# Up projections of both MLPs with tokens as rows, and the squares turned by VectorE in 32x32 blocks

## The chip, the cores and the metric

The kernel runs on one core of a Trainium2 chip. The metric is the device time of one execution in microseconds (us). Engines are named TensorE (PE in profiles), VectorE (DVE), ScalarE (ACT), GpSimd (POOL) and SyncE (SP, which here issues the loads of weights).

## The reference

Two transformer-like layers run one after the other over 256 tokens (S) of width 2048 (D), all in float32. The first mixes a state-space block and an indexed attention, the second a compressed/selected/windowed attention and a gated delta rule. Each ends in an MLP of the same form, which is what the change is about:

```
# first layer                                     # second layer
u = rmsnorm(x, g_mlp) @ w_up                      h = rms_norm(x, ln2_w)
x + jnp.square(jax.nn.relu(u)) @ w_down           x + jnp.square(jax.nn.relu(h @ w_up)) @ w_down
```

w_up is 2048 x 8192, w_down is 8192 x 2048. The result of the second layer goes through one more RMS norm.

## The kernel before, in words

**Products in two parts.** Every float32 factor is split into hi (rounded to fp32r, which TensorE multiplies) and lo (what is left). A product is hi*hi + hi*lo + lo*hi. Activations are held as hi and lo side by side, as tiles of 128 features x 256 tokens (h or mix, [P, 2, 16 * 256]).

**Weights in units.** SyncE loads weights in pieces of 128 x 2048 into a ring of 4 (weight_ring). A piece is two units of 128 x 1024. For each unit ScalarE writes w_hi (a cast, L2115 in split_to) and VectorE then writes w_lo (a subtraction, L1262). There are 4 slots for units (UNITS = 4): ScalarE can cast unit n only when TensorE is done with unit n - 4 (semaphore unit_used), and TensorE takes unit n when VectorE has written its lo (unit_lo). On both engines split_to(unit + UNITS) stands at the head of each step of a stage, and the other work of the step behind it, so an instruction's place in this written order decides what it holds up.

**The MLP's stages.** Each MLP runs in four rounds f = 0 to 3. A round's up stage makes 2048 of the 8192 hidden features, its down stage multiplies them with 2048 rows of w_down and adds to the tokens' x. Each stage takes 32 units, 16 pieces.

- *Up stage before*: features as rows. project -> column -> products_of_two (L531 to L537) keeps 128 x 128 of the weights stationary and moves the activations: 512 columns (hi and lo of 256 tokens) under w_hi, 256 columns (hi) under w_lo. A tile of 128 features is done in two units, and lands in one of banks 0 to 2: hi*hi + lo*hi in the left half and hi*lo in the right. ScalarE lifts the right half (L2121), VectorE adds the left (L1282); for each pair of tiles VectorE does max(.,0) times the norm's 1/root (L1650), ScalarE squares (L2424) and casts the hi part (L2426), VectorE subtracts for the lo part (L1658).
- *Down stage*: tokens as rows. products_moving (L539 to L545) keeps a 128 x 128 piece of the activations stationary (hi, hi, lo) and moves 512 columns of the weights (hi, lo, hi). A block is 512 output features for all 256 tokens; it takes 8 units and two banks (128 tokens each), alternately 3 and 4 or 5 and 6. VectorE adds each bank to the tokens' x (L1726).

The gain of the norm is multiplied in ahead of the up stage (h = x * gain), the 1/root of the mean square behind it. The sum of squares comes from TensorE (folded_norm) as 256 columns, the same on all partitions. In the second MLP the first up stage also turns x into tokens as rows (turned_x: 8 times 4 transposes on TensorE, copied by ScalarE).

## Time and profile before

| | us |
|---|---|
| median of 3 runs | 2675.21 |
| lowest, highest | 2672.89, 2678.63 |
| the profiled execution, its own time | 2677.62 |
| its span | 2675.8 |

| engine | busy us | share of the span | instructions |
|---|---|---|---|
| PE (TensorE, products) | 2642.0 | 99% | 14484 |
| PEld (TensorE, loading what is stationary) | 2274.5 | 85% | 14484 |
| DVE | 1741.5 | 65% | 2361 |
| ACT | 1322.5 | 49% | 1903 |
| POOL | 208.0 | 8% | 182 |

The profile shows one execution. A matmul's recorded length reaches beyond the start of the next one, since they are pipelined, so TensorE's pace is read from the starts of instructions and not from their lengths. The same holds, to a smaller degree, for VectorE and ScalarE. The time of the profiled execution is 1.8 us above its span.

### The profile page before, as it was taken

The numbers are of one execution on the slowest core, as the hardware profiler recorded it, in microseconds if no ns is written. First come the engines' busy times: TensorE is split into PE (matmuls) and PEld (weight loads), VectorE is DVE, ScalarE is ACT, GpSimd is POOL, SyncE is SP. The second block draws the span as 40 slices with busy tenths as digits, with TensorE's granted clock in tenths as the row PEclk, the third lists the DMA queues.
The fourth block names the chain that finished last, engine by engine and source line by source line (L and its number), as shares of the span: only waits on it lengthen the run. The fifth ranks groups of instructions, "written<-read, shape, count | busy, mean of one in ns | idle before, by whom it ended". The sixth has DMA issues, their size and how long they took to land. (4 is left out here: it accounts for less than half of the span.)

```text
span 2675.8 us, 35946 instructions
## 1 busy us (share of the span) xinstructions
PE 2642.0 (99%) x14484; PEld 2274.5 (85%) x14484; DVE 1741.5 (65%) x2361; ACT 1322.5 (49%) x1903; POOL 208.0 (8%) x182
## 2 busy tenths in 40 slices
PE   9999999999999999999999999999999999999998
PEld 8778888888888888888889888988888888888887
DVE  7888796555556555785776767566665555565555
ACT  6545455535445344565554545455555354454454
POOL 3014001000000000140411300000000000000000
PEclk9999999999999999999999999999999999999999
DMA  7644445555555555566333333355555555555553
GB/s 269 165 166 158 164 167 189 189 191 186 198 181 189 203 186 194 186 251 241 142 133 137 125 127 113 131 198 189 189 197 186 198 188 191 189 189 193 185 200 130
DMA packets 68174, 481.91 MB, mean 180 GB/s; under 512 B 8008, under 2 KB 8136, under 8 KB 11177
## 3 DMA queue, kind: packets, MB, share of 16 engines
q1 hardware_dynamic: 65520, 467.43, 48.8%
q0 software_dynamic: 1968, 10.75, 1.5%
q8 instruction: 115, 1.88, 0.3%
q10 hardware_dynamic: 520, 1.43, 0.1%
q14 instruction: 51, 0.41, 0.0%
HBM read 473.29 MB, written 6.29 MB: 179 GB/s over the span
## 5 line engine op out<-in xcount | busy, mean ns | idle before, releaser
L1262 DVE TENSOR_TENSOR w_lo<-weight_ring,w_hi 128x1024 fp32r<-128x1024 f32 x882 | 1083.2, 1238 | 697.8 <-ACT w_hi L2115 696.7
L2115 ACT CAST w_hi<-weight_ring 128x1024 fp32r<-128x1024 f32 x884 | 916.4, 1048 | 646.0 <-PE bank L545 408.9
L533 PE MATMUL bank<-h,w_hi 128*128 128x512 f32 x2848 | 906.9, 400 | 0.0
L536 PEld LDWEIGHTS bank<-h,w_lo 128*128 128x128 f32 x2848 | 535.9, 188 | 126.6
L533 PE MATMUL bank<-mix,w_hi 128*128 128x512 f32 x1776 | 569.8, 402 | 4.1 <-DVE w_lo L1262 1.9
L536 PE MATMUL bank<-h,w_lo 128*128 128x256 f32 x2848 | 560.8, 278 | 0.0
L533 PEld LDWEIGHTS bank<-h,w_hi 128*128 128x128 f32 x2848 | 437.2, 189 | 7.7 <-issue 5.7
L543 PE MATMUL bank<-w_hi,mix 128*128 128x512 f32 x1056 | 411.2, 389 | 0.0
L544 PE MATMUL bank<-w_lo,mix 128*128 128x512 f32 x1056 | 410.9, 389 | 0.0
L545 PE MATMUL bank<-w_hi,mix 128*128 128x512 f32 x1056 | 410.8, 389 | 0.0
L536 PEld LDWEIGHTS bank<-mix,w_lo 128*128 128x128 f32 x1776 | 335.2, 189 | 79.3
L536 PE MATMUL bank<-mix,w_lo 128*128 128x256 f32 x1776 | 350.9, 279 | 0.0
L533 PEld LDWEIGHTS bank<-mix,w_hi 128*128 128x128 f32 x1776 | 272.9, 190 | 7.2 <-DVE w_lo L1262 2.1
L2121 ACT COPY arena<-bank 128x256 f32<-128x256 f32 x274 | 101.6, 372 | 357.3 <-PE bank L536 343.6
L543 PEld LDWEIGHTS bank<-w_hi,mix 128*128 128x128 f32 x1056 | 198.2, 188 | 41.0
L544 PEld LDWEIGHTS bank<-w_lo,mix 128*128 128x128 f32 x1056 | 198.2, 188 | 40.9
L545 PEld LDWEIGHTS bank<-w_hi,mix 128*128 128x128 f32 x1056 | 198.2, 188 | 40.7
L1282 DVE TENSOR_TENSOR arena<-arena,bank 128x256 f32<-128x256 f32 x272 | 113.4, 418 | 130.3 <-ACT arena L2121 130.1
L2797 POOL TENSOR_TENSOR arena<-arena 128x512 f32<-128x512 f32 x28 | 41.6, 1486 | 1067.3 <-ACT arena L2183 1066.5
L2424 ACT ACTIVATE arena<-arena 128x512 f32<-128x512 f32 x64 | 40.4, 632 | 87.9 <-DVE arena L1650 87.9
L1658 DVE TENSOR_TENSOR mix<-arena,mix 128x512 fp32r<-128x512 f32 x64 | 43.9, 685 | 10.8 <-ACT mix L2426 10.8
L1650 DVE SCALAR_TENSOR_TENSOR arena<-arena 128x512 f32<-128x512 f32 x64 | 44.3, 692 | 6.5
(369 smaller groups left out, 1758.9 us busy)
## 6 DMA issues: line engine op xcount, KB each, us to landing
weight_ring<-in_w_up SPq DMA_DIRECT2D x128, 1024.0 KB, 4.8
weight_ring<-in_w_down SPq DMA_DIRECT2D x128, 1024.0 KB, 4.8
weight_ring<-in_w_merge SPq DMA_DIRECT2D x32, 1024.0 KB, 4.8
weight_ring<-in_w_gdn SPq DMA_DIRECT2D x24, 1024.0 KB, 4.8
weight_ring<-in_w_papb SPq DMA_DIRECT2D x16, 1024.0 KB, 4.8
weight_ring<-in_w_o SPq DMA_DIRECT2D x16, 1024.0 KB, 4.8
weight_ring<-in_w_xbc SPq DMA_DIRECT2D x12, 1024.0 KB, 4.8
weight_ring<-in_w_q SPq DMA_DIRECT2D x8, 1024.0 KB, 4.8
```

Source lines behind the costliest of these rows:

```text
L533: e.matmul(bank[:, :], w_hi[:, unit_at % UNITS, o + j * P:o + (j + 1) * P], x[:, :, at + j * S:at + (j + 1) * S], start=first and j == 0, ...
L536: done = e.matmul(bank[:, 0:S], w_lo[:, unit_at % UNITS, o + j * P:o + (j + 1) * P], x[:, 0, at + j * S:at + (j + 1) * S], start=False, st ...
L543: e.matmul(out, x[:, 0, at:at + m], hi, start=first, stop=False)
L544: e.matmul(out, x[:, 0, at:at + m], lo, start=False, stop=False)
L545: return e.matmul(out, x[:, 1, at:at + m], hi, start=False, stop=last)
L1262: e.tensor_tensor(w_lo[:, i, :], ring[:, p % PIECES, half * UNIT:(half + 1) * UNIT], w_hi[:, i, :].bitcast(F32), ALU.subtract).then_inc(un ...
L1282: e.tensor_tensor(dst, dst, bank[:, 0:S], ALU.add).then_inc(read, 1)
L1650: e.scalar_tensor_tensor(out=split(buf, 2), in0=split(buf, 2), scalar=0.0, in1=over(root_m, 2), op0=ALU.max, op1=ALU.mult).then_inc(up_sca ...
L1658: e.tensor_tensor(pair(hid[:, 1, :], n % 8), relu_m[n % 3], pair(hid[:, 0, :], n % 8).bitcast(F32), ALU.subtract).then_inc(up_lo, 1)
L2115: e.copy(w_hi[:, i, :], ring[:, p % PIECES, half * UNIT:(half + 1) * UNIT]).then_inc(unit_hi, 1)
L2121: e.copy(dst, psum[use % 3][0:dst.shape[0], S:2 * S]).then_inc(lifted, 1)
L2797: e.tensor_tensor(sq_total, sq_total, sq_bufs[s % 2], ALU.add).then_inc(res_gathered, 1)
```

## The change

1. **Up stages with tokens as rows.** up_blocks replaces project in the up stages: products_moving with h stationary (128 features x 128 tokens) and 512 columns of w_up moving. Blocks of 512 hidden features take 8 units each and go to banks 3 to 6, as the down stage's do. The weights of w_up are laid out for that (up_tokens), in pieces of the same size.
2. **Relu with the norm.** Tokens are rows now, so 1/root is one number per partition. ScalarE does Relu with that scale straight out of each bank (512 columns) and then squares, for the two halves of a block (relu_squared). The norm's sum is made as one column for each 128 tokens (token_norm).
3. **Turning the squares.** The down stage wants features as rows. VectorE turns the block of 128 tokens x 1024 (two halves of 512 features) with 16 instructions (turn_up): each transposes 32x32 blocks, from 32 partitions of the squares to 32 partitions of the turned buffer, 256 elements on each partition. Then ScalarE casts hi (squared_hi) and VectorE subtracts for lo (squared_lo), 1024 columns each.
4. **Place in the order.** On VectorE 8 of the 16 stand ahead of the split at i = 0 behind each block and 8 ahead of the split at i = 1; squared_lo stands behind the split at i = 2. On ScalarE relu_squared stands ahead of the cast at i = 0 and squared_hi ahead of the cast at i = 3. The last block of an up stage is turned in the first block of the down stage.
5. Turning x in the second MLP moves into block n = 1 of the first up stage and uses banks 0 to 2. The first two columns of an MLP are no longer made in pairs. GpSimd's wait for the end of the first MLP counts blocks (16) in place of pairs of tiles (32).

The diff, cut to its core:

```diff
-        (sqa, sqb, root_m, relu_a, relu_b, relu_c), at = places(0, 512, 512, S, 512, 512, 512)
-        sq_m, relu_m = [sqa, sqb], [relu_a, relu_b, relu_c]
+        (relu0_, relu1_, root_m), _ = places(0, 2 * BLOCK, 2 * BLOCK, 2)
+        (up_turned0, up_turned1), _ = places(10240, 4 * S, 4 * S)
+        relu_m, turned_m = [relu0_, relu1_], [up_turned0, up_turned1]
...
+            def token_norm(i):
+                e.wait_ge(res_gathered, FOLDED * i)
+                for c in range(2):
+                    done = e.matmul(psum[7][:, c:c + 1], sq_total[:, c * P:(c + 1) * P], ones[:, 0:1], start=True, stop=True)
+                done.then_inc(norm_summed, 1)
...
+            def up_blocks(m, f, x):
                 nonlocal unit
                 for n in range(D // BLOCK):
                     b = (4 * m + f) * (D // BLOCK) + n
-                    if m and b < 18:
-                        e.wait_ge(tok_copied, 8)
-                    elif b >= 2:
-                        e.wait_ge(down_added, 2 * (b - 1))
+                    for k in range(KD):
+                        if m and f == 0 and n == 1 and k % 2 == 0:
+                            turned_x(k // 2)
+                        if f == 0 and n == 0:
+                            if k % 2 == 0:
+                                e.wait_ge(xg_lo, gained_x(1 + 2 * m)[1][k])
+                            if k == 12:
+                                token_norm(2 + 2 * m)
+                        if k % 2 == 0:
+                            e.wait_ge(unit_lo, unit + 1)
+                        for c in range(2):
+                            if k == 0 and n >= 2:
+                                e.wait_ge(up_read, 2 * (b - 2) + c + 1)
+                            elif k == 0 and f > 0:
+                                e.wait_ge(down_added, 2 * (b - 2) + c + 1)
+                            done = products_moving(psum[3 + 2 * (n % 2) + c][:, :], unit, (k % 2) * BLOCK, BLOCK, x,
+                                                   k * S + c * P, P, k == 0, k == KD - 1)
+                            if c == 0 and k == KD - 1:
+                                done.then_inc(up_made, 1)
+                        if k % 2:
+                            done.then_inc(unit_used, 1)
+                            unit += 1
...
-                        if n == 0 and k % 2 == 0:
-                            e.wait_ge(up_lo, 8 * (4 * m + f) + k // 2 + 1)
+                        if n == 0 and k % 4 == 0:
+                            e.wait_ge(up_lo, b + k // 4 + 1)
                         if k % 2 == 0:
                             e.wait_ge(unit_lo, unit + 1)
                         for c in range(1 if last and k >= KD // 2 else 2):
-                            done = products_moving(psum[3 + 2 * (b % 2) + c][:, :], unit, (k % 2) * BLOCK, BLOCK, hid,
+                            if k == 0 and n >= 2:
+                                e.wait_ge(down_added, 2 * (b - 2) + c + 1)
+                            elif k == 0:
+                                e.wait_ge(up_read, 2 * (b + 2) + c + 1)
+                            done = products_moving(psum[3 + 2 * (n % 2) + c][:, :], unit, (k % 2) * BLOCK, BLOCK, hid,
...
+            def turn_up(b, i):
+                buf, out = relu_m[b % 2], turned_m[b % 2]
+                if i == 0:
+                    e.wait_ge(up_squared, 2 * (b + 1))
+                for q in (2 * i, 2 * i + 1):
+                    for r in range(4):
+                        src = buf[32 * r:32 * r + 32, :].rearrange("p (c t w) -> p c t w", c=2, t=4)
+                        dst = out[32 * q:32 * q + 32, :].rearrange("p (t c w) -> p c t w", t=4, c=2)
+                        done = e.transpose(dst[:, :, :, 32 * r:32 * r + 32], src[:, :, :, 32 * q:32 * q + 32])
+                done.then_inc(up_turned, 1)
+            def squared_lo(b, hid):
+                e.wait_ge(up_turned, 2 * (b + 1))
+                e.wait_ge(up_hi, b + 1)
+                at = b % 4 * 4 * S
+                e.tensor_tensor(hid[:, 1, at:at + 4 * S], turned_m[b % 2], hid[:, 0, at:at + 4 * S].bitcast(F32),
                                 ALU.subtract).then_inc(up_lo, 1)
...
+            def up_blocks(m, f, hid):
                 nonlocal unit
+                for n in range(D // BLOCK):
+                    b = (4 * m + f) * (D // BLOCK) + n
+                    for i in range(8):
+                        if n > 0 and i < 2:
+                            turn_up(b - 1, i)
                         split_to(unit + UNITS)
                         unit += 1
+                        if f == 0 and n == 0 and i == 7:
+                            e.wait_ge(norm_root, 2 + 2 * m)
+                            e.reciprocal(root_m, root_m).then_inc(norm_rstd, 1)
+                        if n > 0 and i == 2:
+                            squared_lo(b - 1, hid)
...
+                        if n == 0 and i < 2:
+                            turn_up(b + 3, i)
                         split_to(unit + UNITS)
                         unit += 1
+                        if n == 0 and i == 2:
+                            squared_lo(b + 3, hid)
...
+            def relu_squared(b):
+                buf = relu_m[b % 2]
+                if b >= 2:
+                    e.wait_ge(up_turned, 2 * (b - 1))
+                for c in range(2):
+                    if c == 0:
+                        e.wait_ge(up_made, b + 1)
+                    else:
+                        e.wait_ge(unit_used, unit)
+                    e.activation(buf[:, c * BLOCK:(c + 1) * BLOCK], psum[3 + 2 * (b % 2) + c][:, :], ACT.Relu,
+                                 scale=root_m[:, c:c + 1]).then_inc(up_read, 1)
+                for c in range(2):
+                    part = buf[:, c * BLOCK:(c + 1) * BLOCK]
+                    e.wait_ge(up_read, 2 * b + c + 1)
+                    e.activation(part, part, ACT.Square).then_inc(up_squared, 1)
+            def squared_hi(b, hid):
+                at = b % 4 * 4 * S
+                e.wait_ge(up_turned, 2 * (b + 1))
+                e.copy(hid[:, 0, at:at + 4 * S], turned_m[b % 2]).then_inc(up_hi, 1)
...
+            def up_blocks(m, f, hid):
                 nonlocal unit
+                for n in range(D // BLOCK):
+                    b = (4 * m + f) * (D // BLOCK) + n
+                    for i in range(8):
+                        if n > 0 and i == 0:
+                            if f == 0 and n == 1:
+                                e.wait_ge(norm_rstd, 2 + 2 * m)
+                            relu_squared(b - 1)
+                        if n > 0 and i == 3:
+                            squared_hi(b - 1, hid)
                         split_to(unit + UNITS)
                         unit += 1
+                        if f == 0 and n == 0 and i == 7:
+                            e.wait_ge(norm_summed, 2 + 2 * m)
+                            e.activation(root_m, psum[7][:, 0:2], ACT.Sqrt, bias=eps[:, 0:1],
+                                         scale=1.0 / D).then_inc(norm_root, 1)
+                        if m and f == 0 and 8 * n + i in range(9, 17):
+                            turned_copy(8 * n + i - 9)
...
-        "w_up": columns(a["w_up"][0]),
+        "w_up": up_tokens(a["w_up"][0]),
```

Removed lines of the old up stage's evictions are left out above; they are in the functions printed with the kernel. The orders of instructions show what moves. VectorE, before, the start of an up stage with f > 0 (w_lo is the split of a unit, L1282 adds a tile's halves, L1650 scales, L1658 makes the squares' lo part):

```order
L1262 TENSOR_TENSOR w_lo<-weight_ring,w_hi 128x1024 [waits unit_hi_made] x2
L1282 TENSOR_TENSOR arena<-arena,bank 128x256 [waits bank_half_lifted]
L1262 TENSOR_TENSOR w_lo<-weight_ring,w_hi 128x1024 [waits unit_hi_made] x2
L1282 TENSOR_TENSOR arena<-arena,bank 128x256 [waits bank_half_lifted]
L1650 SCALAR_TENSOR_TENSOR arena<-arena 128x512 [waits gemm_bank_read0,gemm_bank_read2]
L1262 TENSOR_TENSOR w_lo<-weight_ring,w_hi 128x1024 [waits unit_hi_made] x2
L1282 TENSOR_TENSOR arena<-arena,bank 128x256 [waits bank_half_lifted]
L1658 TENSOR_TENSOR mix<-arena,mix 128x512 [waits up_hi]
```

Every second split is followed by a short instruction. VectorE, changed kernel, around the end of a block of an up stage (L1290 is the split, L1672 a transpose, L1680 the squares' lo part):

```order
L1290 TENSOR_TENSOR w_lo<-weight_ring,w_hi 128x1024 [waits unit_hi_made] x8
L1672 STREAM_TRANSPOSE arena<-arena 32x2x4x32 [waits up_squared]
L1672 STREAM_TRANSPOSE arena<-arena 32x2x4x32 x7
L1290 TENSOR_TENSOR w_lo<-weight_ring,w_hi 128x1024 [waits unit_hi_made]
L1672 STREAM_TRANSPOSE arena<-arena 32x2x4x32 x8
L1290 TENSOR_TENSOR w_lo<-weight_ring,w_hi 128x1024 [waits unit_hi_made] x2
L1680 TENSOR_TENSOR mix<-arena,mix 128x1024 [waits up_hi,up_turned]
L1290 TENSOR_TENSOR w_lo<-weight_ring,w_hi 128x1024 [waits unit_hi_made] x5
L1672 STREAM_TRANSPOSE arena<-arena 32x2x4x32 [waits up_squared]
```

Now 16 transposes stand in two groups of 8, ahead of the fourth and of the fifth split from the end of the block (the splits of units u+3 and u+4, if the next block begins with unit u), and five splits follow one another undisturbed. ScalarE, before, inside an up stage (L2115 casts a unit, L2121 lifts half a bank, L2424 squares, L2426 casts the squares):

```order
L2115 CAST w_hi<-weight_ring 128x1024 [waits unit_used,piece_loaded0]
L2121 COPY arena<-bank 128x256 [waits unit_used,up_lo]
L2424 ACTIVATE arena<-arena 128x512 [waits up_scaled]
L2426 CAST mix<-arena 128x512 [waits up_squared]
L2115 CAST w_hi<-weight_ring 128x1024 [waits unit_used,piece_loaded0]
L2115 CAST w_hi<-weight_ring 128x1024 [waits unit_used,piece_loaded1]
L2121 COPY arena<-bank 128x256 [waits unit_used,up_lo]
L2115 CAST w_hi<-weight_ring 128x1024 [waits unit_used,piece_loaded1]
L2115 CAST w_hi<-weight_ring 128x1024 [waits unit_used,piece_loaded2]
```

ScalarE, changed kernel, around the end of a block (L2136 casts a unit, L2439 is Relu out of a bank, L2444 Square, L2450 the squares' cast):

```order
L2136 CAST w_hi<-weight_ring 128x1024 [waits unit_used,piece_loaded2]
L2439 ACTIVATE arena<-bank,arena 128x512 [waits up_first_tokens_made,up_turned]
L2439 ACTIVATE arena<-bank,arena 128x512 [waits unit_used]
L2444 ACTIVATE arena<-arena 128x512 [waits up_read] x2
L2136 CAST w_hi<-weight_ring 128x1024 [waits unit_used,piece_loaded2]
L2136 CAST w_hi<-weight_ring 128x1024 [waits unit_used,piece_loaded3] x2
L2450 CAST mix<-arena 128x1024 [waits up_turned]
L2136 CAST w_hi<-weight_ring 128x1024 [waits unit_used,piece_loaded0] x2
L2136 CAST w_hi<-weight_ring 128x1024 [waits unit_used,piece_loaded1] x2
```

The Relu pair and the Squares stand ahead of the cast of unit u+3, and the cast of the turned squares, which waits for all 16 transposes, ahead of the cast of unit u+6. On TensorE the pairs of 512 and 256 columns become products of 512 columns throughout, and a down stage waits for up_lo four times (at its units 0, 2, 4 and 6) in place of eight.

## Rows read from the trace of the kernel before

**Rows 1.** Page, share of the span and instructions of each engine; granted clock in 40 slices
```profile
PE 2642.0 (99%) x14484; PEld 2274.5 (85%) x14484; DVE 1741.5 (65%) x2361; ACT 1322.5 (49%) x1903; POOL 208.0 (8%) x182
PEclk9999999999999999999999999999999999999999
```

**Rows 2.** Windows, 572.8 to 661.8: busy us (instructions) by engine, granted clock, DMA share, GB/s
```profile
572.80:661.80 89.00, 89.00 (x480) 76.55 (x479) 51.38 (x57) 42.39 (x54) 0.00 (x0) 1.00 0.53 185
```

**Rows 3.** Timeline, PE, where the MLPs' stages begin: start us, us, engine, line, operation
```profile
420.79 0.40 PE L527 MATMUL bank<-h,w_hi 128*128 128x512 f32 x1
510.34 0.40 PE L543 MATMUL bank<-w_hi,mix 128*128 128x512 f32 x1
597.41 0.62 PE L533 MATMUL bank<-h,w_hi 128*128 128x512 f32 x2
686.57 0.40 PE L543 MATMUL bank<-w_hi,mix 128*128 128x512 f32 x1
1959.35 0.40 PE L527 MATMUL bank<-h,w_hi 128*128 128x512 f32 x1
2052.49 0.40 PE L543 MATMUL bank<-w_hi,mix 128*128 128x512 f32 x1
```

**Rows 4.** Timeline, PE, inside an up stage and inside a down stage
```profile
655.92 0.63 PE L533 MATMUL bank<-h,w_hi 128*128 128x512 f32 x2
656.62 0.63 PE L533 MATMUL bank<-h,w_hi 128*128 128x512 f32 x2
687.26 0.39 PE L543 MATMUL bank<-w_hi,mix 128*128 128x512 f32 x1
687.94 0.39 PE L543 MATMUL bank<-w_hi,mix 128*128 128x512 f32 x1
```

**Rows 5.** Timeline, PE, v projection, tokens as rows out of h
```profile
160.22 0.39 PE L543 MATMUL bank<-w_hi,h 128*128 128x512 f32 x1
162.94 0.39 PE L543 MATMUL bank<-w_hi,h 128*128 128x512 f32 x1
```

**Rows 6.** Timeline, ScalarE and VectorE, the unit behind the one that ends at 597.41
```profile
597.66 1.05 ACT L2115 CAST w_hi<-weight_ring 128x1024 fp32r<-128x1024 f32 x1 [1.67 <-PE bank L545]
598.75 1.23 DVE L1262 TENSOR_TENSOR w_lo<-weight_ring,w_hi 128x1024 fp32r<-128x1024 f32 x1 [0.29 <-ACT w_hi L2115]
```

**Rows 7.** Groups by line and form: busy us, mean ns, idle before
```profile
L1262 DVE TENSOR_TENSOR w_lo<-weight_ring,w_hi 128x1024 fp32r<-128x1024 f32 x882 | 1083.2, 1238 | 697.8 <-ACT w_hi L2115 696.7
L2278 ACT ACTIVATE arena<-bank 128x512 f32<-128x512 f32 x8 | 4.8, 600 | 2.4 <-PE bank L679 2.4
L2424 ACT ACTIVATE arena<-arena 128x512 f32<-128x512 f32 x64 | 40.4, 632 | 87.9 <-DVE arena L1650 87.9
```

**Rows 8.** Timeline, VectorE and ScalarE, instructions that follow one another without a wait
```profile
612.72 2.36 DVE L1262 TENSOR_TENSOR w_lo<-weight_ring,w_hi 128x1024 fp32r<-128x1024 f32 x2 [2.29 <-ACT w_hi L2115]
1663.66 0.41 DVE L2017 TENSOR_TENSOR arena<-arena,bank 128x256 f32<-128x256 f32 x1
1663.99 0.42 DVE L2012 TENSOR_TENSOR arena<-arena,const_mats 128x256 f32<-128x256 f32 x1
1986.63 0.58 ACT L2445 COPY arena<-bank 128x512 f32<-128x512 f32 x1
1987.11 2.01 ACT L2115 CAST w_hi<-weight_ring 128x1024 fp32r<-128x1024 f32 x2
```

**Rows 9.** Timeline, VectorE, four additions with strided rows of 240 elements
```profile
1180.33 2.02 DVE L1759 TENSOR_TENSOR arena<-arena,vecs 128x240 f32<-128x240 f32 x4
```

**Rows 10.** Timeline, PE, its two long waits for VectorE
```profile
151.49 0.50 PE L543 MATMUL bank<-w_hi,h 128*128 128x512 f32 x1 [1.80 <-DVE w_lo L1262]
1611.46 0.71 PE L1150 MATMUL bank<-arena 128*128 128x128 f32 x4 [1.98 <-DVE arena L2012]
```

**Rows 11.** Busy time and granted clock behind each of these waits
```profile
152.30:155.70 3.40, 3.40 (x10) 2.63 (x9) 3.23 (x12) 1.41 (x2) 0.00 (x0) 0.50 0.93 308
1612.20:1615.00 2.80, 2.80 (x17) 2.15 (x16) 0.06 (x1) 1.71 (x3) 0.00 (x0) 1.00 0.43 178
```

More of the change, by code:

```diff
@@ L232, in mlp @@
         for f in range(FF // D):
[L233 removed]
+            add(up, f * KD, KD)
             add(down, f * KD, KD)
@@ L829, in _, with turned_x @@
             drain(project(KD, mix, 0, 8, (gate_dve, [A[f"lo{k // 4}{k // 2 % 2}"] for k in range(8)])))
-            def turned_x():
-                for b in range(8):
-                    n, c = b // 2, b % 2
-                    yield from rounds(2)
-                    for t in range(4 * n + 1, 4 * n + 4):
-                        bank_done(e, USE["w_o"] + t)
-                    if b >= 4:
-                        e.wait_ge(tok_copied, b - 3)
-                    for j in range(4):
-                        done = e.transpose(psum[3 + b % 4][:, j * P:(j + 1) * P],
-                                           tile(xT, 4 * n + j)[:, c * P:(c + 1) * P], mat("ident"))
-                    done.then_inc(tok_turned, 1)
+            def turned_x(b):
+                n, c = b // 2, b % 2
+                if b == 0:
+                    for t in range(KD):
+                        bank_done(e, USE["w_o"] + t)
+                if b >= 3:
+                    e.wait_ge(tok_copied, b - 2)
+                for j in range(4):
+                    done = e.transpose(psum[b % 3][:, j * P:(j + 1) * P],
+                                       tile(xT, 4 * n + j)[:, c * P:(c + 1) * P], mat("ident"))
+                done.then_inc(tok_turned, 1)
             def turned_back(n):
@@ L2429, in up_tiles @@
-            def up_tiles(first, hid):
-                nonlocal unit
-                for t in range(first, KD):
-                    for i in range(2):
+            def relu_squared(b):
[13 more added lines that the diff above has]
+                    e.activation(part, part, ACT.Square).then_inc(up_squared, 1)
@@ L2472, in mlp @@
             def mlp(m, hid):
-                nonlocal unit
                 for f in range(FF // D):
-                    if f == 0:
-                        split_to(unit + UNITS + 2)
-                        unit += 4
-                        up_tile(0, hid)
-                        up_tile(1, hid)
-                    drain(up_tiles(0 if f else 2, hid), *([turned_copies()] if f == 0 and m else []))
-                    down_blocks(m, f)
+                    up_blocks(m, f, hid)
+                    down_blocks(m, f, hid)
             mlp(0, mix)
@@ L2962, in down_tokens, with up_tokens @@
                                 for f in range(FF // D) for n in range(D // BLOCK)])
+    def up_tokens(w):
+        return _np.concatenate([pieces(w[:, BLOCK * n:BLOCK * (n + 1)], BLOCK) for n in range(FF // BLOCK)])
     mats, hot = constants()
@@ L3003 @@
         "w_o": columns(a["w_o_2"][0]),
-        "w_up2": columns(a["w_up_2"][0]),
+        "w_up2": up_tokens(a["w_up_2"][0]),
         "w_down2": down_tokens(a["w_down_2"][0]),
```

112 lines of the change are left out of this document (26 added, 86 removed).

## The prediction, made before the changed kernel had run

> **What bounds the kernel now.** I read the page first: TensorE is busy for 99% of the span at full clock, VectorE for 65%, ScalarE for 49% [rows 1]. Then the windows of the first MLP: in the 89.0 us from 572.8, TensorE is busy for 89.00, VectorE for 51.4, ScalarE for 42.4 [rows 2]. So inside the MLPs the time is what TensorE needs for its instructions, one behind the other, and nothing else. Third, the timeline of TensorE for where the stages begin and for its pace. An up stage (f > 0) lasts from 597.41 to 686.57, 89.16 us; a down stage lasts from 510.34 to 597.41, 87.07 us [rows 3]. Both stream 32 units of 1024 weight columns. The first up stages are longer: 89.55 us in the first MLP (420.79 to 510.34) and 93.14 in the second (1959.35 to 2052.49, with x being turned in between) [rows 3].
>
> The difference lies in the pace. In the up stage two k tiles (2 x 512 + 2 x 256 moving columns, 1,536 in all) take 0.70 us; in the down stage three products of 512 columns, also 1,536, take 0.68 [rows 4]. Over a whole stage that is 89.16 / 32 = 2.786 us for a unit against 87.07 / 32 = 2.721.
>
> **The change part by part.**
>
> *Products.* The up stages take the form of the down stages: 12 matmuls of 512 columns for a unit in place of 16 (8 of 512 and 8 of 256). Columns stay the same, 6,144. That this form keeps its pace when it reads h, not mix, is seen in the v projection: 12 such matmuls in 2.72 us [rows 5]. So each of the 8 up stages becomes 87.07 us, the first ones with what they have on top: 0.39 us for the norm's sum (89.55 - 89.16) and 3.59 for turning x (93.14 - 89.55). The sum before: 6 x 89.16 + 89.55 + 93.14 = 717.65. After: 8 x 87.07 + 2 x 0.39 + 3.59 = 700.93. **TensorE saves 16.7 us.** The norm's sum becomes two one-column products; I leave it at the 0.39.
>
> *What ScalarE and VectorE do now.* Per block of 8 units ScalarE has two Relu out of a bank, two Squares and one cast of 1024 columns; VectorE has 16 block transposes and one subtraction of 1024. The totals fit: VectorE, 9 subtractions at 1.13 us from start to start (the pair of 2.36 us less one of 1.23) and 16 transposes at e us, 10.2 + 16e, in 8 x 2.72 = 21.8 us. What decides is the burst behind a block, since only 4 units are held split. With T the start of TensorE's first product of the next block, units u, u+1 and u+2 are ready at T; u+3 must be split at T + 3 x 2.72 = 8.16 and u+4 at T + 4 x 2.72 = 10.88. I want both 0.2 us sooner, a margin that I choose for the weight load and the semaphore.
>
> ScalarE starts 0.25 us behind T (597.66 against 597.41) [rows 3, 6]. Relu of the first 128 tokens starts earlier, since its bank is done 0.68 us before T; the second starts at 0.25. Instructions of 512 columns follow each other in 0.48 us (1986.63 to 1987.11) [rows 8]; one lasts 0.60 or 0.63 [rows 7]. So the Squares start at about 0.75 and 1.25 and end at 1.88, and VectorE begins to turn at 1.95. Then in its order: 8 transposes, split of u+3, 8 transposes, split of u+4. u+3 is split at 1.95 + 8e + 1.24, u+4 at 1.95 + 8e + 1.13 + 8e + 1.24 = **4.32 + 16e**. Its ScalarE halves (casts of 1.05 us [rows 6], behind the Squares) are there by T + 4.1.
>
> *The price of one transpose, e.* No STREAM_TRANSPOSE is in this trace. Each moves 256 elements on 32 partitions. The nearest rows are 256-element instructions: 0.41 us long, 0.33 from start to start (1663.66 to 1663.99) [rows 8]. The worst near row is the addition with rows strided by 16 elements: four of 240 elements in 2.02 us, 0.57 for the last, so 0.48 from start to start [rows 9]. The transposes' rows are runs of 32 adjacent elements, so I take the first, **e = 0.33**, and keep 0.48 as the upper end. At the lower end nothing is gained below 0.33, because TensorE is the bound then.
>
> With e = 0.33, u+4 is split at T + 9.6, 1.1 us before the 10.7 I want; u+3 at T + 5.8 against 8.0. Then u+5 at 10.7 (wanted 13.4), the hi copy of the squares on ScalarE at about 8.4 to 9.4, their lo part by T + 12; the down stage wants the last block's squares at its unit 6, T + 16.3. Nothing waits. The limit is e = (10.7 - 4.32) / 16 = 0.40. Beyond it TensorE waits 16 (e - 0.40) us behind each of the 32 up blocks, and the whole gain (16.7 / 32 = 0.52 us a block) is gone at **e = 0.43**.
>
> The page "VectorE: DVE Perf Modes" of the Trainium skill (section "The three transpose paths") gives 311 ns for a VectorE transpose of 128x128 in bf16, and says nothing of fp32. No run here shows it yet. An estimate by that page, with 128 more elements at a cycle each, would be some 0.44 us long and so about 0.36 from start to start, under the limit.
>
> *The rest.* At the first block of each MLP, ScalarE's first Relu waits for the reciprocal of the norm. ScalarE takes the root behind its cast of the block after's third unit, which starts at about T - 2.5 (TensorE is then done with the unit whose slot it fills), so root and reciprocal are there by about T + 0.3 and the Relu pair is well under 1 us late; it fits in the 1.1 of slack. The evictions of the up stage (two half copies, two additions, one scaling per pair of tiles) go; they lay beside TensorE and give back nothing. Banks: a block writes those of two blocks ago, read by Relu 19 us earlier. Weights arrive in the same pieces.
>
> **Sum.** The profiled execution took 2677.6 us (span 2675.8); less 16.7 is 2660.9. It lies 2.4 above the median of the runs, 2675.2. Measured the same way as that, 2675.2 - 16.7 = **2658.5 us**, 0.63% less.
>
> **The rivals.**
>
> *B. A transpose starts only when the one ahead is fully done.* Then the lengths count, not the starts: 1.95 + 8 x 0.42 + 1.24 + 8 x 0.42 + 1.24 = 11.15, so 0.45 us late in each of 32 blocks, 14.4 us: 2658.5 + 14.4 = 2673, no change. Against it: 0.42 long and 0.33 apart in [rows 8], also where the next is of another line. For it: a transpose may have to empty something that an addition doesn't.
>
> The Trainium skill has such a rule: "VectorE: DVE Perf Modes", section "The DRAIN you can't avoid", says that a following op doesn't start until the pipe is empty. By that rule this rival's 2673 would be the time if the recorded length were the spacing; the trace disagrees for additions, with 0.33 us between starts of 0.41 us instructions.
>
> *C. Transposes are slow: slower than before.* At e = 0.48, u+4 is split at T + 12.0, 1.3 us late, times 32 is 42 us: 2658.5 + 42 = 2700. It decides from e = 0.43 on. A wait can also cost the clock: behind the wait of 1.80 us at 151.49 TensorE ran for 3.4 us at a granted clock of 0.50, the 1.2 GHz level, while behind that of 1.98 us at 1611.46 it stayed at full clock [rows 10, 11]. 3.4 us at half pace lose 1.7 us; if every block's wait did so, 54 more, 2755. For C: 16 short instructions of a kind that the trace doesn't show, on a quarter of the partitions, written across blocks. Against it: none of the near rows is so slow without a stride on the single element.
>
> *D. The pace doesn't change*: the up stages keep 2.79 us a unit and the time stays at 2675. [Rows 5] speak against it.
>
> **How the numbers follow.** A (forecast) 0.60, B 0.12, C 0.22, D 0.06. A alone lies in 2655 to 2662 (the runs of before spread by 3 us to either side). The range goes up into C: 2654 to 2695 leaves out some 0.17 of C above and 0.03 below. 0.2% is 5.4 us, about what a measurement can tell. Faster: all of A and the third of B with e between 0.40 and 0.41, 0.64. The same: the rest of B and nearly all of D, 0.13. Slower: C and a crumb, 0.23.
>
> **What would show it.** In the profile after: up stages of 87.1 us, a step from start to start of the transposes at 0.40 us or less, VectorE's split of the fifth unit behind each block ending at least 0.2 us before TensorE takes it, and no wait of TensorE for w_lo in the MLPs. Waits of TensorE for w_lo at unit u+4 of every block, 32 of them, would mean B or C, and their length gives e; half-clock stretches behind them would mean C's second part. Waits at another place (for the squares in a down stage, for a bank, for the norm) would make the prediction wrong in a way that I have priced at nothing.

## The result, and the profile after

| kernel | median us (lowest to highest) | ratio to before, 95% interval |
|---|---|---|
| before, same chip | 2674.05 (2672.88 to 2678.63) | |
| changed | 2689.45 (2689.04 to 2691.06) | 1.0052 [1.004, 1.0065] |

The change makes the kernel 15.4 us slower; the forecast was 16.7 us faster. The time lies inside the predicted range, but on the other side of the kernel before. The profiled execution has a span of 2689.3 us at a mean granted clock of 0.997.

The page of the changed kernel (share of the span by engine; granted clock in 40 slices):

```profile
PE 2631.4 (98%) x13464; PEld 2223.0 (83%) x13464; DVE 1866.3 (69%) x2649; ACT 1312.2 (49%) x1807; POOL 206.7 (8%) x182
PEclk9999999999999999999999999999999999999999
```

Against [rows 1] TensorE has 1,020 instructions less and 10.6 us less of busy time, and yet the span grew. So the time is in idle stretches of TensorE, and the view of its waits names them (us in total, times, longest):

```profile
PE bank L544 <- DVE w_lo L1290: 25.5, 33, 1.5
```

L1290 is the split of a unit. Two of the 33 are in the v projection (2.9 us in e1 below, where only they are left). The other 31 are in the MLPs: every block of an up stage but one is followed by one. The first block of the second MLP is spared: in the block behind it TensorE also turns x, takes 3.2 us for a unit in place of 2.72, and so comes to unit u+4 later.

Where the stages begin, on TensorE's timeline (start us, us, engine, line, operation), which answers to [rows 3]:

```profile
600.60 0.39 PE L544 MATMUL bank<-w_hi,h 128*128 128x512 f32 x1
...
690.59 0.39 PE L544 MATMUL bank<-w_hi,mix 128*128 128x512 f32 x1
...
778.69 0.39 PE L544 MATMUL bank<-w_hi,h 128*128 128x512 f32 x1
```

The up stage with f > 0 takes 89.99 us (89.16 before, 87.07 forecast). The down stage takes 88.10 (87.07 before): the fourth block of an up stage is turned in the down stage's first block, so it has one late unit as well. The window of the up stage answers to [rows 2]:

```profile
600.60:690.60 90.00, 87.94 (x386) 71.85 (x385) 63.49 (x85) 43.28 (x48) 0.00 (x0) 1.00 0.53 187
```

TensorE is idle for 2.06 of the 90.00 us, at full clock. VectorE is busy for 63.5 of them, so on the mean it has time; it is late at one place in each block. That place, on ScalarE's and VectorE's timelines behind the block end T = 645.10 (the last column is the idle time before, and what ended it):

```profile
644.68 1.31 ACT L2439 ACTIVATE arena<-bank,arena 128x512 f32<-128x512 f32 x2 [1.00 <-PE bank L546]
645.89 1.14 ACT L2444 ACTIVATE arena<-arena 128x512 f32<-128x512 f32 x2
...
647.06 3.57 DVE L1672 STREAM_TRANSPOSE arena<-arena 32x256 f32<-32x256 f32 x8 [2.12 <-ACT arena L2444]
650.66 1.23 DVE L1290 TENSOR_TENSOR w_lo<-weight_ring,w_hi 128x1024 fp32r<-128x1024 f32 x1
651.92 3.60 DVE L1672 STREAM_TRANSPOSE arena<-arena 32x256 f32<-32x256 f32 x8
655.55 2.36 DVE L1290 TENSOR_TENSOR w_lo<-weight_ring,w_hi 128x1024 fp32r<-128x1024 f32 x2
```

The transposes begin at T + 1.96, as forecast (T + 1.95). Eight of them take 3.57 us where 8 x 0.33 had been forecast. The split of unit u+3 starts at T + 5.56; that of u+4 starts at T + 10.45 and takes 1.23, so it ends at T + 11.68 = 656.78. It was due at T + 4 x 2.72 = T + 10.88, when TensorE is through with the four units before it. TensorE's timeline there:

```profile
645.10 0.39 PE L544 MATMUL bank<-w_hi,h 128*128 128x512 f32 x1
...
655.75 0.39 PE L546 MATMUL bank<-w_hi,h 128*128 128x512 f32 x1
656.83 0.50 PE L544 MATMUL bank<-w_hi,h 128*128 128x512 f32 x1 [0.69 <-DVE w_lo L1290]
657.16 0.39 PE L545 MATMUL bank<-w_lo,h 128*128 128x512 f32 x1
657.39 0.40 PE L546 MATMUL bank<-w_hi,h 128*128 128x512 f32 x1
```

The product at 656.83 was due at 655.98 (0.227 behind the one at 655.75): 0.85 us late. The next one follows in 0.33, not 0.227, which is 0.10 more. By the stage, a block loses (89.99 - 87.04) / 3 = 0.98 us, with 87.04 for a stage without waits (e1). 31 x 0.98 = 30.4 of the 31.2 us that lie between the changed kernel and e1. Two of the 31 waits are longer: 1.02 us behind the first block of the first MLP, where Relu also waits for the norm's reciprocal, and 0.92 behind the second block of the second MLP, where ScalarE also copies the turned x.

The groups of the changed kernel by line and form (busy us, mean ns, idle before) answer to [rows 7]:

```profile
L1672 DVE STREAM_TRANSPOSE arena<-arena 32x256 f32<-32x256 f32 x512 | 223.2, 436 | 76.2 <-ACT arena L2444 69.1
...
L2439 ACT ACTIVATE arena<-bank,arena 128x512 f32<-128x512 f32 x64 | 41.8, 688 | 31.6 <-PE bank L546 30.1 <-DVE arena L1694 1.4
L2444 ACT ACTIVATE arena<-arena 128x512 f32<-128x512 f32 x64 | 36.5, 623 | 0.0
```

A transpose is 436 ns long, little more than the 256-element additions of [rows 8] (0.41 to 0.42). It is the step from start to start that differs most: (3.57 - 0.436) / 7 = 0.448 us, against their 0.33.

### The profile page after: what moved, and what is told of

Same layout as the page of the kernel before. It is cut to its first block and busy times, and to the rows that moved or that the text cites. A ratio compares the mean times of both kernels' runs of the same rounds, so it can differ in the third digit from the quotient of the medians.

```text
span 2689.3 us, 33854 instructions
## 1 busy us (share of the span) xinstructions
PE 2631.4 (98%) x13464; PEld 2223.0 (83%) x13464; DVE 1866.3 (69%) x2649; ACT 1312.2 (49%) x1807; POOL 206.7 (8%) x182
## 5 line engine op out<-in xcount | busy, mean ns | idle before, releaser
L1290 DVE TENSOR_TENSOR w_lo<-weight_ring,w_hi 128x1024 fp32r<-128x1024 f32 x882 | 1080.8, 1238 | 592.7 <-ACT w_hi L2136 589.6
L2136 ACT CAST w_hi<-weight_ring 128x1024 fp32r<-128x1024 f32 x884 | 919.5, 1048 | 771.0 <-PE bank L546 634.8
L544 PE MATMUL bank<-w_hi,h 128*128 128x512 f32 x1056 | 415.5, 393 | 19.2 <-DVE w_lo L1290 19.2
L545 PE MATMUL bank<-w_lo,h 128*128 128x512 f32 x1056 | 411.3, 389 | 0.0
L546 PE MATMUL bank<-w_hi,h 128*128 128x512 f32 x1056 | 411.2, 389 | 0.0
L534 PE MATMUL bank<-h,w_hi 128*128 128x512 f32 x864 | 281.9, 408 | 0.0
L1672 DVE STREAM_TRANSPOSE arena<-arena 32x256 f32<-32x256 f32 x512 | 223.2, 436 | 76.2 <-ACT arena L2444 69.1
L544 PEld LDWEIGHTS bank<-w_hi,h 128*128 128x128 f32 x1056 | 198.2, 188 | 71.0 <-DVE w_lo L1290 30.5
L546 PEld LDWEIGHTS bank<-w_hi,h 128*128 128x128 f32 x1056 | 198.2, 188 | 41.8
L545 PEld LDWEIGHTS bank<-w_lo,h 128*128 128x128 f32 x1056 | 198.3, 188 | 40.1 <-issue 0.2
L537 PEld LDWEIGHTS bank<-h,w_lo 128*128 128x128 f32 x864 | 162.6, 188 | 38.3
L537 PE MATMUL bank<-h,w_lo 128*128 128x256 f32 x864 | 170.4, 279 | 0.0
```

The lines of the kernel that those rows point to most:

```text
L534: e.matmul(bank[:, :], w_hi[:, unit_at % UNITS, o + j * P:o + (j + 1) * P], x[:, :, at + j * S:at + (j + 1) * S], start=first and j == 0, ...
L537: done = e.matmul(bank[:, 0:S], w_lo[:, unit_at % UNITS, o + j * P:o + (j + 1) * P], x[:, 0, at + j * S:at + (j + 1) * S], start=False, st ...
L544: e.matmul(out, x[:, 0, at:at + m], hi, start=first, stop=False)
L545: e.matmul(out, x[:, 0, at:at + m], lo, start=False, stop=False)
L546: return e.matmul(out, x[:, 1, at:at + m], hi, start=False, stop=last)
L1290: e.tensor_tensor(w_lo[:, i, :], ring[:, p % PIECES, half * UNIT:(half + 1) * UNIT], w_hi[:, i, :].bitcast(F32), ALU.subtract).then_inc(un ...
```

## The experiments

The theory after the result: TensorE's new pace is as forecast, and the whole loss is one late unit, because 16 transposes stand ahead of the split of u+4 and one comes 0.45 us behind another. The rivals: the waits are a price of the burst as a whole (ScalarE's part in it too), so that moving instructions only moves the wait; and the pace itself has a hidden cost.

**e1: the second group one unit later.** VectorE's order only; nothing is taken away.

```diff
-                        if n > 0 and i < 2:
-                            turn_up(b - 1, i)
+                        if n > 0 and i in (0, 2):
+                            turn_up(b - 1, i // 2)
```

(and the same in the down stage)

> The two groups of 8 transposes stand ahead of the splits at i = 0 and i = 2, not 0 and 1; nothing else changes. Theory S (the order: the split of u+4 stands behind 16 transposes of 0.45 us, all other deadlines have room): u+4 split at T + 8.1 (wanted 10.9), u+5 at T + 12.9 (wanted 13.6), the squares' lo part at T + 14.1 (the down stage wants it at T + 16.3). No wait of TensorE for w_lo in the MLPs, up stages of 87.1 us, 2657 to 2661 us, 30 less than the changed kernel and 15 less than the one before. Rival W (16 transposes of 0.45 us are too much work behind a block, wherever they stand): the wait moves to u+5, u+6 or to up_lo in the down stage, and the time stays at 2680 to 2690.

Measured: 2658.27 us (2656.87 to 2659.85), ratio 0.9939 [0.9926, 0.9951]. VectorE and TensorE's waits for w_lo in the projections:

```profile
640.62 3.57 DVE L1672 STREAM_TRANSPOSE arena<-arena 32x256 f32<-32x256 f32 x8 [2.12 <-ACT arena L2444]
644.22 2.36 DVE L1290 TENSOR_TENSOR w_lo<-weight_ring,w_hi 128x1024 fp32r<-128x1024 f32 x2
646.61 3.60 DVE L1672 STREAM_TRANSPOSE arena<-arena 32x256 f32<-32x256 f32 x8
650.24 1.23 DVE L1290 TENSOR_TENSOR w_lo<-weight_ring,w_hi 128x1024 fp32r<-128x1024 f32 x1
```

```profile
PE bank L544 <- DVE w_lo L1290: 2.9, 2, 1.5
```

The same 16 transposes at the same 0.45 us, and no wait is left in the MLPs. With T = 638.66, u+4 is now split by 646.58 (T + 7.9) and u+5 by 651.47 (T + 12.8), due at 5 x 2.72 = T + 13.6. The stage, on TensorE's timeline:

```profile
595.14 0.39 PE L544 MATMUL bank<-w_hi,h 128*128 128x512 f32 x1
...
682.18 0.39 PE L544 MATMUL bank<-w_hi,mix 128*128 128x512 f32 x1
```

87.04 us, where 87.07 had been forecast. So the pace, and that nothing else is late, are shown, and this version is faster than both kernels (e1's interval against the kernel before lies wholly below 1).

**e2: four transposes ahead of each of the first four splits**, squared_lo and squared_hi one unit later.

```diff
-                        if n > 0 and i < 2:
+                        if n > 0 and i < 4:
                             turn_up(b - 1, i)
...
-                for q in (2 * i, 2 * i + 1):
+                for q in (i,):
```

> Four transposes ahead of each of the splits at i = 0, 1, 2, 3; squared_lo behind the split at i = 3, squared_hi ahead of the cast at i = 4. Theory S: splits of u+3, u+4, u+5, u+6 end at T + 5.0, 8.1, 11.1, 14.1 (wanted 8.2, 10.9, 13.6, 16.3), the squares' lo part at T + 15.3, 1.0 ahead of the down stage's unit 6. The same as the groups at 0 and 2: 2657 to 2661. Rival W: waits at several places, 2680 or more.

Measured: 2658.31 us (2656.73 to 2662.86), 0.9942 [0.9928, 0.9955]: the same as e1. Two different orders in which each split comes in time give the same gain.

**e3: only the first 8 transposes.**

```diff
-                    for r in range(4):
+                    for r in range(4 if i == 0 else 0):
```

(the semaphore up_turned is then raised by 2 behind the first group; the other half of the squares is not turned)

> Leaves out the second group of 8 transposes (half of the squares are not turned), all else in its place. Theory S: u+4 split at T + 1.95 + 8 x 0.45 + 2.4 = 8.0, no wait, 2657 to 2661, the floor that TensorE sets. If the time is above 2665, TensorE's up stages cost more than 87.1 us for another reason (rival: pace).

Measured: 2659.68 us, 0.9945 [0.9931, 0.9959]. Half of the transposes gone gives no more than moving them (e1): what counts is their place ahead of one split, not their sum.

**e4: 18 transposes ahead of the split of u+4** (the two added ones write a spare place).

```diff
+                if i == 1:
+                    for r in range(2):
+                        ...
+                        done = e.transpose(dst, src[:, :, :, 0:32])
                 done.then_inc(up_turned, 1)
```

> Two more transposes of the same shape behind the second group of 8, into a spare buffer (18 in all). Theory S: each instruction past the limit costs its spacing 0.45 us in each of the 32 blocks, 14.4 us: 2689.5 + 28.7 = 2718, with waits of TensorE of about 1.6 us at u+4. Rival L (only the length of the wait, the clock or something periodic counts): if waits of 1.6 us cost the clock in every block, 1.7 us each, 2770; if the transposes are not on the path, 2690.

Measured: 2720.72 us (2715.98 to 2722.84), 1.0169 [1.0155, 1.0183], 31.3 above the changed kernel. Two more at 0.45 in 32 blocks are 28.8. By the stages they cost (92.76 - 89.99) / 3 = 0.92 us a block, 28.6 in 31 blocks; the rest lies within the spread of e4's own runs, 6.9 us. TensorE's waits, one of them on its timeline, and the window behind it (busy us by engine, granted clock, DMA share, GB/s):

```profile
PE bank L544 <- DVE w_lo L1290: 53.5, 33, 1.9
```

```profile
637.78 0.50 PE L544 MATMUL bank<-w_hi,h 128*128 128x512 f32 x1 [1.58 <-DVE w_lo L1290]
```

```profile
637.60:641.60 4.00, 3.82 (x17) 3.15 (x18) 4.00 (x5) 2.54 (x3) 0.00 (x0) 1.00 0.40 137
```

The number of waits stays and their length grows by the transposes added. Waits of 1.58 us in nearly every block left the granted clock at 1.00, and so did the longest two in the MLPs, of 1.91 and 1.81 us.

**e5: Square of 32 columns only**, so that the transposes start earlier (the rest of the squares is left out).

```diff
-                    e.activation(part, part, ACT.Square).then_inc(up_squared, 1)
+                    if c:
+                        e.activation(part[:, 0:32], part[:, 0:32], ACT.Square).then_inc(up_squared, 2)
```

> The changed kernel, but ScalarE squares only 32 columns of a block (the rest of the squares is left out), so VectorE can begin to turn about 0.9 us sooner; the transposes and their order are untouched. Theory S (it is the length of the chain Relu, Squares, 8 transposes, split, 8 transposes, split): u+4 is split at T + 10.8 in place of 11.7, TensorE waits next to nothing, 2658 to 2663. Rival V (VectorE's transposes slow the splits or TensorE by themselves): 2689 as before.

Measured: 2668.98 us (2668.01 to 2672.79), 0.9975 [0.9965, 0.9984]. An earlier start gives 20.5 us back, as the mechanism wants, but the time is 6 us above the expectation's upper end. The splits, and TensorE at u+4 of the block with T = 641.29:

```profile
651.05 2.36 DVE L1290 TENSOR_TENSOR w_lo<-weight_ring,w_hi 128x1024 fp32r<-128x1024 f32 x2
```

```profile
651.95 0.39 PE L546 MATMUL bank<-w_hi,h 128*128 128x512 f32 x1
652.33 0.50 PE L544 MATMUL bank<-w_hi,h 128*128 128x512 f32 x1
652.66 0.39 PE L545 MATMUL bank<-w_lo,h 128*128 128x512 f32 x1
```

The split ends at 652.28, 0.1 behind the due 652.17. TensorE starts 0.15 late and its next product comes 0.33 behind, with no wait in the list of waits for this block: 0.25 us by these rows, and by the stages (87.96 - 87.04) / 3 = 0.31 us a block, 10 in all. A unit that is 0.1 us late costs 0.3.

**e6: a copy in place of each transpose**, same places, same order (nothing is turned).

```diff
-                        done = e.transpose(dst[...], src[...])
+                        done = e.tensor_copy(dst[...], src[...])
```

> The changed kernel with a copy in place of each transpose, of the same 256 elements from and to the same places (so nothing is turned). Theory Q (the reordering itself keeps an instruction from overlapping the next): copies start 0.33 us or less apart, no wait of TensorE, 2657 to 2661. Rival P (32 partitions, or the crossing from one quarter of the partitions to another, cost it): copies start 0.45 apart, 2689.

Measured: 2658.4 us, 0.9935 [0.992, 0.9949]. The group of the copies and one of their runs:

```profile
L1672 DVE COPY arena<-arena 32x256 f32<-32x256 f32 x512 | 145.8, 285 | 76.3 <-ACT arena L2444 69.1
```

```profile
640.78 2.36 DVE L1672 COPY arena<-arena 32x256 f32<-32x256 f32 x8 [2.12 <-ACT arena L2444]
```

The time fits the idea that the transposition itself forbids the overlap, but the row doesn't: the copies are only 285 ns long, and (2.36 - 0.285) / 7 = 0.296 us apart, so that they don't overlap either. What the copies share with the transposes is the form and the places.

**e7, e9, e10: other forms in the same slots** (a block's number picks the form; the squares are turned wrongly or in part). They are read by their rows. Each was run once, 2672.63, 2661.16 and 2671.91 us, and these times mix several forms. e7 tries adjacent elements, fewer elements, and 128 partitions:

```diff
+                elif form == 2:
+                    ... e.transpose(out[32*q:32*q+32, 256*r:256*r+128], buf[32*r:32*r+32, 256*q:256*q+128])
+                else:
+                    ... e.transpose(out[:, at:at + n], buf[:, at:at + n])   # 128 partitions, n = 256, 128
```

> One look at the length and the spacing of other forms of the transpose, by block in turn of four: the form of the change; 32 x 256 adjacent elements to adjacent ones; 32 x 128; 128 partitions x 256 and x 128 (the squares are turned wrongly or in part). Theory Q: spacing = length + 0.01 for each, length = a fixed 0.17 us + a cycle for each element, so 0.44, 0.44, 0.30, 0.44, 0.30. Rival P: the adjacent form or the one on 128 partitions overlaps as additions do, 0.33 apart for 256.

A quarter is a group of 32 partitions, 0 to 31, 32 to 63 and so on. e9 reads and writes the same quarter, then 64 partitions, then copies, then the change's own transposes with the two loops exchanged, then 128 partitions:

```diff
+                if form == 0:
+                    ... e.transpose(out[32*q:32*q+32, w], buf[32*q:32*q+32, w])       # 4 in each quarter
+                elif form == 3:
+                    ... e.tensor_copy(out[32*q:32*q+32, w], buf[32*q:32*q+32, w])
+                elif form == 4:
+                    for r in A:
+                        for q in B: ...        # the written quarter changes each time
```

> One look at spacing, by block in turn of six (the squares are turned wrongly or in part): transposes of 256 elements on 32 partitions within their own quarter; on 64 partitions; copies on 64; copies on 32 within their quarter; the transposes of the change in another order (the written quarter changes with every instruction); transposes and copies on 128 partitions. If the small number of partitions costs the overlap, both kinds on 32 are spaced by their length plus 0.01, wherever they write, and those on 128 by less than their length. If crossing costs it, the ones within their own quarter overlap (0.35 apart for transposes). 64 partitions are open.

e10 takes crossing a quarter and changing quarters apart:

```diff
+                if form == 0:      # 4 in a row from quarter a to another quarter q
+                elif form == 1:    # own quarter, another one each time
+                elif form == 2:    # quarter q + 1 to q, another pair each time
+                else:              # 64 partitions, half to half, 4 in a row
```

> One look at spacing, by block in turn of four (the squares are turned wrongly or in part), all transposes of 256 adjacent elements on 32 partitions: the same crossing four times in a row (0 to 1, 2 to 3, and back); own quarter, but another quarter at each instruction; crossing, another pair at each instruction; and on 64 partitions from one half to the other. If crossing costs the overlap: 0.45, 0.35, 0.45, and 0.45 or so on 64. If the change of quarters from one instruction to the next costs it: 0.35 (but one of 0.45 in 8), 0.45, 0.45, 0.35.

| instructions | mean length ns | a run | mean from start to start, us |
|---|---|---|---|
| transposes 32x256, as in the change | 436 | 8 in 3.57 | 0.448 |
| the same, adjacent elements (e7) | 436 | 8 in 3.57 | 0.448 |
| 32x128 (e7) | 303 | 8 in 2.51 | 0.315 |
| 128x256 (e7) | 424 | 2 in 0.77 | 0.35 |
| the change's, written quarter changing (e9) | 436 | 8 in 3.58 | 0.449 |
| 32x256, own quarter, 4 in each (e9) | 404 | 8 in 2.84 | 0.335 within a quarter |
| 32x256 across, same pair 4 in a row (e10) | 404 | 8 in 2.84 | 0.335 within a pair |
| 32x256, own quarter, another each time (e10) | 436 | 8 in 3.59 | 0.45 |
| 32x256 across, another pair each time (e10) | 436 | 8 in 3.59 | 0.45 |
| 64x256, 4 in a row (e9, e10) | 410 | 4 in 1.42 | 0.34 |

The rows of e7 (as in the change, 128 elements, 128 partitions):

```profile
645.29 3.57 DVE L1678 STREAM_TRANSPOSE arena<-arena 32x256 f32<-32x256 f32 x8 [2.12 <-ACT arena L2461]
...
668.03 2.51 DVE L1683 STREAM_TRANSPOSE arena<-arena 32x128 f32<-32x128 f32 x8 [2.12 <-ACT arena L2461]
...
689.79 0.77 DVE L1689 STREAM_TRANSPOSE arena<-arena 128x256 f32<-128x256 f32 x2 [2.12 <-ACT arena L2461]
```

Two transposes on 128 partitions overlap (0.77 us for two that are 0.42 long on the mean): the transposition doesn't forbid it. The rows of e9 (own quarter, copies in their own quarter, the change's with the loops exchanged):

```profile
665.06 2.84 DVE L1674 STREAM_TRANSPOSE arena<-arena 32x256 f32<-32x256 f32 x8 [2.12 <-ACT arena L2469]
...
511.73 1.79 DVE L1687 COPY arena<-arena 32x256 f32<-32x256 f32 x8 [2.12 <-ACT arena L2469]
...
620.53 3.58 DVE L1693 STREAM_TRANSPOSE arena<-arena 32x256 f32<-32x256 f32 x8 [2.12 <-ACT arena L2469]
```

On 32 partitions too they overlap, as do the copies (8 in 1.79, not 2.36). With the loops exchanged it is the written quarter that changes each time; in the change it is the quarter that is read. Either is enough. The rows of e10, in the order of its forms:

```profile
445.47 2.84 DVE L1674 STREAM_TRANSPOSE arena<-arena 32x256 f32<-32x256 f32 x8 [2.37 <-ACT arena L2459]
466.90 3.59 DVE L1678 STREAM_TRANSPOSE arena<-arena 32x256 f32<-32x256 f32 x8 [2.12 <-ACT arena L2459]
489.57 3.59 DVE L1682 STREAM_TRANSPOSE arena<-arena 32x256 f32<-32x256 f32 x8 [2.12 <-ACT arena L2459]
512.36 1.42 DVE L1687 STREAM_TRANSPOSE arena<-arena 64x256 f32<-64x256 f32 x4 [2.12 <-ACT arena L2459]
```

Crossing from one quarter to another costs nothing if the instruction before took the same way. What costs is an input or an output that starts in another quarter than that of the instruction before; then the one starts only when the other is done. Taken one by one, the eight of such a run of e10 start at 621.16, 621.52, 621.85, 622.18, 622.58, 622.95, 623.28 and 623.60. The step at the change of quarters is 0.40 us, the length of the one before (0.39) and 0.01. The steps without a change are 0.36 or 0.37 behind an instruction that was itself held (0.43 to 0.44 long) and 0.32 to 0.33 behind the others (0.39 to 0.40 long); 0.335 is their mean. Where every instruction is held, each is 0.436 long and the step is 0.449.

e10 also ties the row to the time. All its blocks of 32 partitions have 16 transposes of 256 elements in the same places of VectorE's order, only the routes differ. TensorE's list of waits for w_lo has 18 entries, 13.3 us: two in the v projection and one behind each of the 16 blocks in which every instruction changes quarter (0.57 or 0.69 us, once 0.80). Behind the 8 blocks with the same pair four times in a row there is none, nor behind the 8 on 64 partitions. In e7 and e9 too it waits in the MLPs only behind the blocks that have 8 in 3.57 or 3.58.

**e8: groups ahead of the splits of u+4 and u+5.**

```diff
-                        if n > 0 and i < 2:
-                            turn_up(b - 1, i)
+                        if n > 0 and i in (1, 2):
+                            turn_up(b - 1, i - 1)
```

> The two groups of 8 transposes ahead of the splits at i = 1 and i = 2. The chain of deadlines as measured so far (transposes 0.45 apart; a split 1.23 long; TensorE late if a split ends after the unit's time, plus 0.2 to 0.3 for a first product without its load ahead): u+3 split at T + 4.1, u+4 at T + 9.0 (wanted 10.9), u+5 at T + 13.9 (wanted 13.6): late by 0.3 in each of 32 blocks, 0.5 with the restart, 2658 + 16 = 2674, with the waits at the sixth unit of a block, not the fifth. If only the fifth unit matters (rival): 2658.

Measured: 2671.43 us (2667.3 to 2673.8), 0.9982 [0.9973, 0.9992]. The split of u+5 of the block with T = 619.23, and TensorE there:

```profile
631.75 1.23 DVE L1290 TENSOR_TENSOR w_lo<-weight_ring,w_hi 128x1024 fp32r<-128x1024 f32 x1
```

```profile
632.60 0.39 PE L546 MATMUL bank<-w_hi,h 128*128 128x512 f32 x1
633.03 0.50 PE L544 MATMUL bank<-w_hi,h 128*128 128x512 f32 x1
633.37 0.40 PE L545 MATMUL bank<-w_lo,h 128*128 128x512 f32 x1
```

Now u+5 is the late one: its split ends at 632.98 and it was due at 632.83. 13.2 us above e1 are 0.41 a block; by the stages (88.06 to 88.17 us against 87.04) it is 0.34 to 0.38, and the rest is within the spread of the runs. So u+4 isn't special: the rule is the due time of each unit against all that stands ahead of its split.

## Why the prediction was wrong, by its own steps

**Products: right.** The stages without waits take 87.04 us against 87.07, and the kernel with the change's whole work and no late unit (e1) takes 2658.27 against the 2658.5 forecast. The two first up stages take 87.57 and 91.51 us there, where 87.46 and 91.05 had been forecast, 0.6 us more in all. Rival D is refuted.

**When the transposes start: right.** T + 1.96 against T + 1.95. A Relu is 0.69 us long where 0.60 had been taken, but the Squares still end at T + 1.93 (forecast 1.88). Of "the rest", no wait for banks or for the squares' lo part shows in the MLPs. The norm's reciprocal was to make the first Relu a little late, within the slack of 1.1 us; it did (the first block's wait is 0.33 us longer), and since the slack was gone, it cost that.

**The price of one transpose, e = 0.33: this step failed.** It is 0.449 us from start to start, above both the limit of 0.40 and the 0.43 at which the whole gain is gone. The prediction's own formula was sound: with 0.449, 4.32 + 16e = T + 11.5, measured T + 11.68. Most of the rest is that the second group is held behind the split as well (650.66 to 651.92, 1.26 where 1.13 stood): it writes quarter 2, the split quarter 0. The value was drawn from [rows 8], additions that all start in the same quarter as the one before. Not one of the rows quoted had an instruction whose quarters differ from its predecessor's, and the length of the nearest row (0.41 to 0.42) already lay above the limit of 0.40. A step whose limit lies between the spacing and the length of the nearest row turns wholly on the overlap, and that was taken over from rows of another form.

**Rival B: the mechanism, with a length and a price too small.** "A transpose starts only when the one ahead is fully done" is what happens, wherever the quarter changes. B counted steps of 0.42 and 0.45 us lost per block, 2673. The real step is a length of 0.436 and 0.013 between. That puts the split at T + 11.68 and not at 11.15, and against the 10.7 that the prediction wanted it is 0.98 us, just what a block loses: 0.98 x 31 = 30.4 on 2658.5 is 2688.9, measured 2689.45. So the margin of 0.2, chosen without a row, was borne out: a split that ends 0.1 (e5), 0.15 (e8) or 0.80 us (the change) behind its due time costs 0.31, 0.34 to 0.38 and 0.98. B was argued against with rows of additions and given 0.12.

The Trainium skill, "VectorE: DVE Perf Modes", section "Two Vector instructions with no wait between them", states the rule as measured here: a Vector instruction is held until all earlier ones are finished if an input starts in another quadrant (32 partitions) than the last read, or the output in another than the last written. All runs agree, 0.449 us held against 0.335 not held. The prediction weighed the section "The DRAIN you can't avoid" of the same page instead. Read as a general rule it disagrees with additions (0.33) and with transposes in one quarter (0.335), and agrees with held instructions alone. The section itself exempts a next op that is not held, which the prediction left out.

**Rival C: its condition came true, its price and its clock did not.** It was to decide from e = 0.43 on, and e is 0.449, so the kernel is slower, to which the prediction gave 0.23. But e is not 0.48, and no wait of up to 1.9 us in the MLPs lowered the clock (e4). Of what C named, the short instructions on a quarter of the partitions don't cost the overlap (e9, e10), and adjacent elements are as slow as the writing across blocks (e7); the cause is B's. That 2689 lies inside the stated range is owed to the width of the range, which reached into C; the mechanism that was forecast did not hold.

## What to carry to other kernels

Turned as here, by 16 instructions on 32 partitions with 16 different pairs of quarters, 128 partitions leave no two instructions with the same pair in any order, so each counts with its full length, 0.45 us for 256 fp32 elements; take the spacing of overlapping rows only where input and output stay in their quarters. Whether fewer and wider instructions could do part of the turn (on 64 and 128 partitions they came 0.34 to 0.35 us apart) wasn't tried. Where an engine feeds another through a short queue, compute for each unit when it is due and what stands ahead of it; here moving 8 instructions behind one more split, with no work removed, is worth 31 us, and leaves 16.4 us of gain. Leave each due time some room, since a unit 0.1 us late costs 0.3; 0.7 us was enough (u+4 behind the blocks of e9 and e10 in which 8 transposes take 2.84), and where between the two it begins to cost isn't shown.

## What the runs showed of the hardware that was not expected

- VectorE: a change of quarter from one instruction to the next costs about 0.12 us for 256 elements in transposes where each is held (0.449 against 0.33) and 0.09 in copies (0.296 in e6 against 0.20 to 0.21 in e9). The number of partitions (32, 64 or 128) hardly matters: the mean lengths of 404, 410 and 424 ns differ mostly because the first of a run is longer (0.43 to 0.45) and weighs more in a short one; the others are 0.39 to 0.40 long.
- TensorE, taken up behind a late operand: its first product is followed after 0.33 us, not 0.227, also where the list of waits shows no wait (e5, e8).
- TensorE's clock: behind the wait of 1.80 us in [rows 10, 11] the granted clock was 0.50; behind the 31 waits of e4 in the MLPs (mostly 1.58 us, up to 1.91) it stayed at 1.00, the 2.4 GHz level. It did so too behind the same wait of the v projection in e9, 1.84 us long. So the length of the wait alone doesn't decide it; what does wasn't tried.
